# Gate and up weights of every expert pair in the ring, split by contraction instead of by expert, in a mixture-of-experts trunk

## What is computed

```python
def expert_step(acc, ew):
    wg, wu, wd, gcol = ew            # (1024,256) (1024,256) (256,1024), gate column
    h = jax.nn.silu(xt @ wg) * (xt @ wu)
    return acc + gcol[:, None] * (h @ wd).astype(F32), None
```

## Time and profile before

| what | value |
|---|---|
| median of three runs | 1608.55 us (1607.81 to 1611.89) |
| the profiled execution: its own time, its span | 1611.03 us, 1609.2 us |
| granted TensorE clock, mean | 0.992 |
| busy share of the span: PE, PE weight loads, DVE, ACT, POOL | 97%, 49%, 33%, 21%, 9% |
| chain that ended last: PE, DMA, DVE | 84%, 8%, 5% |
| moved by the DMA queues | 536.18 MB, of which SP's queue 470.88 MB |
| DMAs of 1 MB from the gate, up and down weights into the ring | 124 each |
| their median time from issue to landing | 13.5, 16.5 and 15.0 us |
| MoE stages, from first to last `gate_up` | 184.6 to 660.3 us and 1078.8 to 1556.4 us |

### The profile page before, as it was taken

One profiled execution on the slowest core, in us unless ns is written; L12 is line 12 of the kernel. 1 busy time (PEld: TensorE's weight loads), 2 busy tenths in 40 slices (PEclk: granted clock), 3 DMA queues, 4 the chain that ended last, 5 costly groups with the idle time before them and its releaser, 6 DMA issues.

```text
span 1609.2 us, 22408 instructions
## 1 busy us (share of the span) xinstructions
PE 1562.5 (97%) x8258; PEld 793.3 (49%) x8258; DVE 537.7 (33%) x1328; ACT 339.4 (21%) x688; POOL 149.0 (9%) x241
## 2 busy tenths in 40 slices
PE   7999899999999999999999999989999999999998
PEld 5775544344444443466665754554443444444435
DVE  2157522222222222351434335462222122222226
ACT  2211122121221221221222221022211122122222
POOL 0241100000000000000111011020000000000000
PEclk9999999999999999999999999999999999999999
DMA  9733999999989999973577586589999998999990
GB/s 293 271 115 152 361 402 420 420 421 419 419 362 420 420 420 419 386 264 105 177 241 242 192 281 236 200 344 403 421 420 420 414 417 352 421 420 420 421 366 30
DMA packets 121756, 536.18 MB, mean 333 GB/s; under 512 B 17897, under 2 KB 29545, under 8 KB 73936
## 3 DMA queue, kind: packets, MB, share of 16 engines
q1 hardware_dynamic: 98599, 470.88, 73.6%
q0 software_dynamic: 21216, 61.12, 10.5%
q10 hardware_dynamic: 1872, 3.22, 0.6%
HBM read 526.15 MB, written 23.87 MB: 342 GB/s over the span
## 4 chain that ended last, share of the span: by engine, by line
PE 84%; DMA 8%; DVE 5%; issue 1%; ACT 1%; SPq 1%; DVEq 0%; POOLq 0%; ACTq 0%
PE ps L1373 24%; PE ps L1402 12%; PE ps L1157 11%; PE ps L1187 9%; DMA weights<-in_w_exp_up 7%; PE ps L1313 6%; PE ps L1366 4%; PE ps L1309 2%; PE ps L1386 2%; PE ps L1395 1%; PE ps L1066 1%; DVE x_tok L2491 1%; PE ps L1563 1%; PE ps L1330 1%; PE ps L1044 1%
## 5 line engine op out<-in xcount | busy, mean ns | idle before, releaser
L1373 PE MATMUL ps<-weights,x_feat 128*64 128x512 f32 x1856 | 408.9, 593 | 10.9 <-DMA weights<-in_w_exp_up 8.4
L1373 PEld LDWEIGHTS ps<-weights,x_feat 128*64 128x64 f32 x1856 | 134.6, 137 | 276.0 <-issue 276.0
L1402 PE MATMUL ps<-weights,arena 128*64 128x512 f32 x992 | 226.5, 599 | 0.9 <-ACT arena L1593 0.9
L1157 PE MATMUL ps<-x_feat,weights 128*128 128x288 f32 x800 | 203.6, 412 | 1.1 <-ACT x_feat L1593 1.1
L1157 PEld LDWEIGHTS ps<-x_feat,weights 128*128 128x128 f32 x800 | 154.3, 195 | 43.6 <-issue 3.8
L2247 DVE CAST split<-state 128x1024 fp32r<-128x1024 f32 (+1 forms) x66 | 44.7, 677 | 325.0 <-ACT state L1593 325.0
L2244 DVE SCALAR_TENSOR_TENSOR arena<-arena,ps 128x256 f32<-128x256 f32 x64 | 30.8, 481 | 348.7 <-ACT arena L1823 348.7
L2644 POOL DMA_INDIRECT arena<-x_rows,arena x64 | 63.6, 994 | 876.7 <-DVE arena L2237 833.4
L1593 ACT ACTIVATE state<-ps 128x512 f32<-128x512 f32 x132 | 78.8, 597 | 283.6 <-PE ps L1402 261.2
L1402 PEld LDWEIGHTS ps<-weights,arena 128*64 128x64 f32 x992 | 65.7, 136 | 132.2 <-issue 130.9
L1823 ACT ACTIVATE arena<-ps 128x256 f32<-128x256 f32 x64 | 24.5, 383 | 430.7 <-PE ps L1373 404.3
(11 more groups left out here) (311 smaller groups left out, 1323.9 us busy)
## 6 DMA issues: line engine op xcount, KB each, us to landing
weights<-in_w_exp_gate SPq DMA_DIRECT2D x124, 1024.0 KB, 13.5
weights<-in_w_exp_up SPq DMA_DIRECT2D x124, 1024.0 KB, 16.5
weights<-in_w_exp_down SPq DMA_DIRECT2D x124, 1024.0 KB, 15.0
weights<-in_w_in_c SPq DMA_DIRECT2D x24, 1024.0 KB, 7.7
arena<-in_state_ret POOLq DMA_DIRECT2D x20, 512.0 KB, 5.2
out_ret_sample<-arena POOLq DMA_DIRECT2D x20, 512.0 KB, 6.4
weights<-in_w_in_a SPq DMA_DIRECT2D x8, 1024.0 KB, 10.2
weights<-in_w_ple_gate SPq DMA_DIRECT2D x8, 1024.0 KB, 18.1
```

Source lines behind the costliest of these rows:

```text
L1157: last = pe.matmul(ps[:, 0:T], lhs(c), XT[:, c, :], start=(c == 0), stop=(c == n - 1))
L1373: last = pe.matmul(ps[64 * s:64 * s + 64, :], XGT[u][:, c, 64 * s:64 * s + 64], rhs, start=(c == 0), stop=(c == KC - 1))
L1402: last = pe.matmul(ps[64 * s:64 * s + 64, :], HT[u][:, c, 64 * s:64 * s + 64], wd[s][:, c, 512 * n:512 * n + 512], start=(c == 0), stop=(c ...
```

## The change

It does five things. `contraction_panel` takes an expert number that is a loop register as well. SP uses it for panels 0 and 1 of every ring pair, the preloaded second pair included. SP issues panel 0 of pair P when the first half of `gate_up` of pair P - 2 has ended (a count that PE now raises in every ring pair), and panel 1, as before, when the whole has. PE takes every ring pair with `gate_up_halves`, so it begins with panel 0 alone and waits for panel 1 in the middle. The waits for both panels ahead of `gate_up` are gone. The matmuls are the same in number and shape, and panel 2 is untouched.

```diff
                     for m, w in enumerate((A["w_exp_gate"], A["w_exp_up"])):
-                        src = w[l, e0:e0 + 2].rearrange("e (p c) n -> p e (c n)", c=KC)
+                        pair = w[l, e0:e0 + 2] if isinstance(e0, int) else w[l, bass.ds(e0, 2)]
+                        src = pair.rearrange("e (p c) n -> p e (c n)", c=KC)
...
                         wait_slot(n0 + 3 * pr + k)
-                        if pr == 0 and k < 2:
-                            contraction_panel(k + n0, 0, k)
+                        if k < 2:
+                            contraction_panel(n0 + 3 * pr + k, 2 * pr, k)
...
-                            elif isinstance(it, int) and it == 1 and u + k == 0:
-                                sp.wait_ge(sem("half_consumed"), l + 1)
+                            elif k == 0:
+                                sp.wait_ge(sem("half_consumed"), (PAIRS - 1) * l + 2 * it + u - 1)
                             else:
                                 sp.wait_ge(bank_full[0], base[0] + 2 * (u + late) - 3 + 4 * it)
-                            if isinstance(it, int) and it > 1 and k < 2:
-                                contraction_panel(n0 + 6 * it + k, 4 * it, k)
+                            if k < 2:
+                                contraction_panel(n0 + 3 * u + k, 4 * it + 2 * u, k)
...
-                        if it == 0:
+                        if isinstance(it, int) and it == 0 and u == 0:
                             emptied(pe, (f"rows{l}", k))
...
-                        if it == 0 and k == 0:
+                        if k == 0:
                             last.then_inc(sem("half_consumed"), 1)
...
-                        elif not (first or last):
-                            for n in range(ring, ring + 2):
-                                pe.wait_ge(slot_full[n % SLOTS], 32 * (n // SLOTS + 1) + 32 * it)
...
-                        if first or last:
+                        if home:
+                            gate_up(u, HOME_UP, PS[:, 0, :]).then_inc(bank_full[0], 1)
+                        else:
                             gate_up_halves(u, ring, it, PS[:, 0, :]).then_inc(bank_full[0], 1)
-                        else:
-                            gate_up(u, HOME_UP if home else [wp(ring), wp(ring + 1)], PS[:, 0, :]).then_inc(bank_full[0], 1)
```

## The result

The changed kernel takes 1621.37 us in the median of four runs (1619.82 to 1623.07), the kernel before 1609.13 us beside it (1607.81 to 1611.89): a ratio of 1.0066 on record, 95% interval 1.0049 to 1.0083 (the two medians by themselves give 1.0076). The forecast of 1606 us was wrong, its range to 1617 us too, and the sign. The profiled spans are 1621.3 and 1609.2 us, so there are 12.1 us to explain, or 14.7 us against the forecast's -2.6.

What follows compares the result with a forecast made beforehand. PE's chain was taken as the bound, with 12.4 us of stalls for up weights; less stall in stretch A against more in stretch B gave -0.8 and -1.8 us a layer, together -2.6: 1608.55 to 1606 us, range 1599 to 1617.

Steps and rivals of the forecast that it cites:

- stretch B: From the home pair to the stage's end: 1.1 us more stall in the first layer, 0.1 us more in the second.
- the 5.5 (6.5) us in which the ring stood full: After the home pair: loading time lost with a full ring, 5.5 us first layer, 6.5 second, usable to absorb lag.
- the 1.2 us at the stage's start: Start of each layer's MoE stage: asking for panel 0 sooner returns 1.2 us a layer of lost loading.
- stretch A: Pairs 2 to 11, up to `shared_down`: 1.9 us less stall a layer, 3.1 to 1.2 and 4.0 to 2.1 us.
- The signs that it named as right: MoE stages: 408 to 413 GB/s, later stalls, no dip after the home pair, SP issues of several us every pair.
- Rows of 4 KB: Ring pairs' gate and up loads: 409 GB/s against 420.5, so 0.28 us more loading a pair.
- The rival in which the rows cost nothing: Ring pairs: short rows cost no rate, all 12.4 us of stalls come back, 1596 us; chance 0.11.
- The slower rival: Ring pairs: rate falls to 402 GB/s when every pair has short rows, +7.5 us, 1616 us; chance 0.17.
- The later deadline: Ring pairs' `gate_up`: panel 1 may land 3.5 us later, room gained once for each stretch, not for each pair.
- Costs at nothing: PE's split wait, SP's third wait and held issues, and the later embedding gate panels add no time while the queue is full.

Runs made afterwards that it cites:

- the kernel before with the even order: The kernel before with the gather's slots permuted so that the fetched token rows spread over all partitions: 1605.55 us, ratio 0.9974; the changed kernel with it: 1611.34 us.
- the rows alone: The changed kernel with both waits put back as before, so that rows of 4 KB are the only change: 1624.09 us, ratio 1.0088.
- The half wait alone: The changed kernel with the old release of panel 0 (after the whole `gate_up`); rows of 4 KB and the half wait stay: 1624.25 us, ratio 1.0093.
- the packed order: The changed kernel with the gather's slots in another order, meant to fill some DMA engines with up to 8 rows and leave others empty: 1642.70 us, ratio 1.0200.
- the kernel with the change in its first part alone: The kernel before with the change for pairs 2 to 11 only; from pair 12 on all is as before: 1612.77 us, ratio 1.0018.

## Why the prediction was wrong, step by step

**The step that failed** is in stretch B: "which eat 3.3 of the 5.5 (6.5) us in which the ring stood full", "so the remaining 2.2 (3.2) us are used too. The loads then start 2.2 (3.2) us earlier". Next to nothing of it was left at the stream's end. The first loads after the home pair were asked for 3.3 us sooner, at 446.4 us against 449.7, and the four of them had landed 3.0 us later. Before, then after:

```profile
L748 SPq DMA_DIRECT2D weights<-in_w_exp_up x2: 377/490/604, 450.1 to 451.1; - x2
...
DMA to landing us min/median/max: 4.8/9.3/12.7
```

```profile
L758 SPq DMA_DIRECT2D weights<-in_w_exp_up x2: 414/422/429, 446.9 to 450.3; - x2
...
DMA to landing us min/median/max: 8.1/12.6/16.5
```

451.1 + 12.7 = 463.8 us before, 450.3 + 16.5 = 466.8 after. With the 1.2 us at the stage's start the prediction took back 6.7 and 7.7 us a layer; by the streams 7.8 - 7.6 = 0.2 and 7.8 - 7.4 = 0.4 us came back. The two differences, 6.5 and 7.3, make 13.8 of the 14.7 us. In PE's time it is stretch B that lost most: it grew by 6.1 and 4.7 us where 1.1 and 0.1 were forecast, 9.6 us off, and stretch A is 4.3 us off.

The rate of 362 GB/s at a share of 0.89 is a mean over 16 engines. It was read as 5.5 us in which the queue had room; most of that was room of engines that were ahead. Before the change the last panel ahead of the gap in the loads, in which PE works on the home pair, landed at 428.5 + 20.0 = 448.5 us, and the next load was asked for at 449.7: the last engine had only just ended.

The landings also show that the net of 0.2 and 0.4 us hides two errors. Counted from the stage's start, the changed kernel's stream is 4.0 and 6.7 us behind with the last down panel ahead of the gap, 2.7 and 3.5 us with the first down panel behind it, and 7.6 and 7.4 us at the end. So 1.3 and 3.2 us did come back at the gap, and the twelve pairs behind it then cost 0.41 and 0.33 us each at the last landing, where 0.28 was taken. Why the last engine's price is higher there is open; the spread between the engines grows in the same stretch.

That a mean can hide this was not among the rivals, and the range had no case in which the reserve is worth nothing, though a dip in a mean rate has 0 as its lower bound. With it the prediction's own sums give 1606 + 5.5 + 6.5 = 1618 us, and 1620 with the start's 1.2 us a layer at nothing too. The signs that it named as right, 408 to 413 GB/s and no dip after the home pair, came true while the time did not: they were signs of the mean rate.

**Rows of 4 KB: right in the mean rate.** 412 GB/s instead of the 409 taken. That 7.8 us a layer were forecast and the stream is 7.6 and 7.4 us longer is in part luck, by the two errors above. The rival in which the rows cost nothing fell: 412 GB/s against 420. The Trainium skill's 512 bytes as the smallest transfer for line rate ("DMA: Bandwidth & Descriptors", Specifications) don't agree with the trace here either: rows of 4 KB moved at 412 GB/s, rows of 8 KB at 420. The slower rival's rate of 402 GB/s did not come either; its 1616 us lay nearer for another reason.

**Stretch A: hardly any of the gain came.** A gain of 1.9 us a layer was forecast. Pair 12 begins 184.90 us after the stage's start in the first layer and 1272.15 - 1085.34 = 186.81 in the second, where it was 185.10 and 1264.83 - 1078.76 = 186.07: 0.2 us less, 0.7 more. In the first layer the stretch's last wait is for panel 1 of pair 11. It ended at 346.83 us before and at 350.42 after, 3.2 us later in the stage; the forecast let 2.8 - 1.2 = 1.6 us through. The later deadline's 3.5 us is worth what it was taken for and covers just that.

In the second layer the first pair's `gate_up` took 8.79 us where it had taken 7.09: the granted clock was 0.64 in 1085 to 1088 us, so for part of it at the lower level (1.2 GHz), after 5 us in which PE had been busy for 3.1. This doesn't go with the change: from the first pair to the second it is 15.1 us here and 15.0 in the kernel before with the even order (1074.97 to 1089.93 us, granted clock 0.50 in 1075 to 1078 us), and 13.4 with the rows alone (1085.70 to 1099.13) as in the kernel before. Whether it has a part in the 0.7 us was not shown.

**The later deadline: right only inside the stage.** It moves a wait to the middle of `gate_up` and lets PE begin sooner. At the end of the stage it has no use, since the last things needed, the down panel and what comes after it, have no halves. The half wait alone brought nothing that the runs can tell.

**Costs at nothing: right.** SP was held for up to 7.11 us in one issue, beside 412 GB/s; such holds came in the later pairs, not in every pair as the prediction's signs had it. The embedding gate's first user waits 0.24 us, and for ACT, as before; only it begins 6.3 us later. The split wait adds 441.6 - (408.9 + 28.2) = 4.5 us of PE time, of which 1.7 are the second layer's first pair at the lower clock; the rest was not broken down. Where PE waits for the stream this costs nothing.

## What to carry to other kernels

A transfer is there when the slowest of the 16 engines has done its part, so a dip in the mean DMA rate can be counted as a reserve only as far as the engines are evenly loaded; give it zero as a lower bound, and look at the time from issue to the last landing before and after the dip. A small gather beside a full weight stream can set the pace by which partitions its valid rows lie in: spreading them cost one table and was worth 4 us in the kernel before, and 10 us in the changed one, where the queue never ran empty. And where a stage ends with the last landing of a stream, a later deadline or an earlier request inside it is worth only what it takes out of the stream's idle time.

## What the runs showed of the hardware that was not expected

The order of some 72 rows of 4 KB in a pair (two experts of 36 tokens), under 5% of its bytes (0.3 MB beside 6.3 MB of weights), moved the time of the whole kernel by 31 us between the even and the packed order (1611.3 and 1642.7 us). A fuller queue let the spread between the engines grow: it fell back to 2.5 us at the home pair in the kernel before, and reached 12.6 us where the queue never ran empty. That the fuller queue is the cause was not tested by itself: in the kernel with the change in its first part alone, the first layer's stream is 0.9 us behind the kernel before two pairs after the gap and 2.7 us at its end, though the two load the same way there.
